# Sparse-attention phase of a hybrid decoder step: packed weights for the prompt blocks, head columns copied tile by tile, first prompt units amid the gate rows, decode softmax in quarters

## The reference

```python
h = rms_norm(x, prm['norm_g'])
p_m, p_n, p_r, p_c = _split(h @ prm['w_in'], GROUP_SIZES)
y_m, ... = mlstm_mixer(p_m, ...)        # group A: matrix memory
y_n, ... = nsa_mixer(p_n, ...)          # group B: sparse attention
y_r, ... = rwkv_mixer(p_r, ...)         # group C: RWKV-7
y_c = memory_mixer(p_c, mem_kv, prm)    # group D: cross attention to 256 memory tokens
y = jnp.concatenate([y_m, y_n, y_r, y_c], -1) @ prm['w_out']
return x + y, ...
```

```python
for r in range(R):                       # R = 2 halves of a block of 32
    hid = hid + jnp.einsum('bnshcd,csde->bnhce', sub[:, r:r + n_cmp],
                           w1[:, r * CMP_STRIDE:(r + 1) * CMP_STRIDE])
kv = jnp.einsum('bnhce,ced->bnhcd', jax.nn.gelu(hid), prm['nsa_cmp_w2'])
...
e = jnp.exp(s - jnp.where(jnp.isfinite(m), m, 0.0))
return e / jnp.maximum(jnp.sum(e, -1, keepdims=True), 1e-30)
...
o = gt[:, :, 0] * o_cmp + gt[:, :, 1] * o_slc + gt[:, :, 2] * o_win
out = o.reshape(B, T, GW).astype(p.dtype) * jax.nn.silu(z)
```

## Time and profile before

| | us |
|---|---|
| median of three runs (lowest, highest) | 1641.11 (1629.98, 1643.89) |
| profiled execution, its own time | 1643.66 |
| span in the profile | 1642.0 |
| PE busy | 1446.8 (88%) |
| DVE busy | 809.4 (49%) |
| ACT busy | 406.2 (25%) |
| POOL busy | 169.3 (10%) |
| chain that ended last, by engine | PE 72%, DVE 11%, issue 8%, SP queue 3%, ACT 2%, DMA 2% |
| granted TensorE clock, mean | 0.895 |

### The profile page before, as it was taken

One profiled execution on the slowest core, in us unless ns is written; L12 is line 12 of the kernel. 1 busy time (PEld: TensorE's weight loads), 2 busy tenths in 40 slices (PEclk: granted clock), 3 DMA queues, 4 the chain that ended last, 5 costly groups with the idle time before them and its releaser, 6 DMA issues.

```text
span 1642.0 us, 28050 instructions
## 1 busy us (share of the span) xinstructions
PE 1446.8 (88%) x9880; PEld 1032.9 (63%) x9880; DVE 809.4 (49%) x2006; ACT 406.2 (25%) x783; POOL 169.3 (10%) x312
## 2 busy tenths in 40 slices
PE   5998989889998988678999899999989989877787
PEld 3774877888854765354458377788877548644443
DVE  1445557665455635742125466665463475266411
ACT  4230102111112344530332110121110124336300
POOL 0000000000000263220000000000000003651100
PEclk9987899996799988899999779999586989888999
DMA  7132322510031465255242233131100404571611
GB/s 298 66 105 65 135 86 65 168 52 1 1 136 60 131 175 184 74 206 216 77 157 77 80 103 132 52 105 78 52 2 1 160 35 152 155 236 33 245 65 64
DMA packets 93216, 175.91 MB, mean 107 GB/s; under 512 B 14114, under 2 KB 79827, under 8 KB 86931
## 3 DMA queue, kind: packets, MB, share of 16 engines
q1 hardware_dynamic: 80066, 124.58, 22.9%
q0 software_dynamic: 13008, 49.54, 8.6%
HBM read 161.27 MB, written 21.12 MB: 111 GB/s over the span
## 4 chain that ended last, share of the span: by engine, by line
PE 72%; DVE 11%; issue 8%; SPq 3%; ACT 2%; DMA 2%; POOL 0%; POOLq 0%; DVEq 0%; ACTq 0%
PE bank L581 16%; PE bank L618 12%; PE bank L1186 8%; PE bank L2743 3%; PE bank L514 2%; PE bank L1320 2%; SPq L387 2%; PE bank L2259 2%; PE bank L814 1%; PE bank L1212 1%; PE bank L1308 1%; PE bank L1297 1%; PE bank L2283 1%; DMA stream<-in_slcV 1%; DVE area L1663 1%
## 5 line engine op out<-in xcount | busy, mean ns | idle before, releaser
L581 PE MATMUL bank<-stream,hT 128*128 128x512 f32 (+3 forms) x768 | 266.9, 505 | 14.6 <-ACT area L594 14.1
L618 PE MATMUL bank<-hT,stream 128*128 128x272 f32 x960 | 229.8, 401 | 5.1 <-DVE area L1552 5.1
L581 PEld LDWEIGHTS bank<-stream,hT 128*128 128x128 f32 x768 | 148.4, 197 | 117.1 <-issue 103.2
L618 PEld LDWEIGHTS bank<-hT,stream 128*128 128x128 f32 x960 | 185.6, 194 | 44.8 <-DVE area L1552 5.3
L1186 PE MATMUL bank<-stream,prm 128*128 128x256 f32 x512 | 127.5, 412 | 0.4 <-DVE YT L1533 0.4
L2743 PE MATMUL bank<-stream,YT 128*128 128x512 f32 x256 | 114.3, 608 | 5.6 <-DVE YT L2651 5.6
L1186 PEld LDWEIGHTS bank<-stream,prm 128*128 128x128 f32 x512 | 105.8, 209 | 18.3 <-issue 1.4
L2259 PE MATMUL bank<-cst,hT 128*128 128x128 f32 x224 | 44.7, 318 | 55.1 <-DVE hT L2715 54.5
L2743 PEld LDWEIGHTS bank<-stream,YT 128*128 128x128 f32 x256 | 49.5, 195 | 68.0 <-issue 61.9
L407 POOL DMA_DIRECT2D stream<-in_slcV x128 | 68.8, 542 | 129.7 <-PE bank L2241 68.9
L2259 PEld LDWEIGHTS bank<-cst,hT 128*128 128x128 f32 x224 | 25.4, 150 | 87.4 <-DVE hT L2715 81.9
(11 more groups left out here) (616 smaller groups left out, 2357.9 us busy)
## 6 DMA issues: line engine op xcount, KB each, us to landing
stream<-in_cmpL SPq DMA_DIRECT2D x256, 128.0 KB, 2.3
stream<-in_win_ SPq DMA_DIRECT2D x12, 2048.0 KB, 8.0
stream<-in_slcK SPq DMA_DIRECT2D x128, 64.0 KB, 2.3
stream<-in_slcK POOLq DMA_DIRECT2D x128, 64.0 KB, 2.5
stream<-in_slcV SPq DMA_DIRECT2D x128, 64.0 KB, 2.6
stream<-in_slcV POOLq DMA_DIRECT2D x128, 64.0 KB, 2.7
stream<-in_wout SPq DMA_DIRECT2D x4, 2048.0 KB, 9.0
out_winpast<-in_winraw POOLq DMA_DIRECT2D x2, 4064.0 KB, 26.6
```

The costliest lines, as they stand in the source:

```text
L581: last = nc.tensor.matmul(ps[:, 0:w], hT[:, k, tok(i)], ws[:, k, :], start=(k == 0), stop=(k == KT - 1))
L618: last = nc.tensor.matmul(ps[:, 0:HALF], ws[:, k, 128 * f:128 * f + 128], hT[:, k, HALF * s:HALF * s + HALF], start=(k == 0), stop=(k == K ...
```

## The change

It has four parts.

1. **Packed weights.** The weights `w1p`, which the decode pages are compressed with already, serve the prompt blocks too. `KVT` holds pairs of neighbouring tokens in the two halves of the partitions, and 8 matmuls take the place of 16 for each of keys and values. w1f is no longer streamed.
2. **Heads by tile.** ACT copies T3 tile by tile (`act_take_heads`), tile 0 in phase R, behind a new wait for the store of the shift rows (`so`); the others ahead of the barrier. The memset of the tail rows and the GELU of `HIDD` move into phase R. PE does `pe_r_end` before the last tile of T3.
3. **First units amid the gate rows.** Scores of units 0 and 1 come before F3's fourth row block, and their maxima and exponentials are taken there; units 0 and 1 get buffers of their own. The selection of the decode blocks comes later on DVE.
4. **Decode softmax.** DVE masks the selected scores by quarters, each with its maximum (`dve_decode_mask`), at units 0, 1, 3 and 4. ACT takes the exponential in three steps at units 5 to 7. The selected scores are no longer scaled before the transposes; instead the value products are scaled as they are added. Window scores move to unit 1, memory scores to unit 3, turns to `TSTEP`, values to a new `VSTEP`.

POOL's loads of slcK 0 and 1 come ahead of its stores of new cache rows.

```diff
-            items += [("w", l, n) for n in ("T2", "T3", "T4", "T5")] + [("w1f", l), ("w", l, "F3")]
+            items += [("w", l, n) for n in ("T2", "T3", "T4", "T5", "F3")]
@@ pool_r
-            pool.dma(f"stR{l}", pool.eng.dma_start(io["rsh"][l], SHO).then_inc(stored["R"][l], 16))
+            pool.dma(f"so{l}", pool.eng.dma_start(io["rsh"][l], SHO).then_inc(shift_stored[l], 16), "so", l)
@@ act_r
             act(nc.scalar.copy(TK, bank("dtk", l)[:, 0:128]).then_inc(act_done, 1), "TK", l)
+            act.wait_ge(dve_done, at("HID", l, DB - 1))
+            act.wait_ge(dve_done, at("peb", l))
+            for c in range(2):
+                act(nc.scalar.activation(HIDD[:, :, c, :], HIDD[:, :, c, :], ACT.Gelu_apprx_tanh, bias=peb[:, c:c + 1]).then_inc(act_done, 1), "G", l)
...
+            act.wait_ge(shift_stored[l], at("so", l))
+            act.wait_ge(pe_done, at("full", "dbn", l))
+            act.wait_ge(dve_done, at("ntails", l))
+            act_take_heads(act, l, 0)
             act.wait_ge(dve_done, at("v20", l))
@@ dve_r
             dve_r_dec(dve, l)
+            dve(nc.vector.memset(PN[:, 4, 0:1166], 0.0).then_inc(dve_done, 1), "ntails", l)
             dve_r_norm(dve, l)
@@ pool_n
+            pool_pages(pool, "slcK", l, 0)
+            pool_pages(pool, "slcK", l, 1)
             pool.wait_ge(act_done, at("PT4", l))
...
-            for kind in ("slcK", "slcV"):
-                for c in range(4):
-                    pool_pages(pool, kind, l, c)
+            pool_pages(pool, "slcK", l, 2)
+            pool_pages(pool, "slcK", l, 3)
+            for c in range(4):
+                pool_pages(pool, "slcV", l, c)
@@ pe_n
-            pe_project_tm(pe, l, "T3")
-            pe_r_end(pe, l)
+            pe.wait_ge(sem_of_slot("w", l, "T3"), at("here", "w", l, "T3"))
+            for i in range(TILES):
+                if i == 4:
+                    pe_r_end(pe, l)
+                pe_project_tile(pe, l, "T3", i)
+            pe.name("used", "w", l, "T3")
...
-            pe_project_rows(pe, l, "F3", 3)
+            pe.wait_ge(dve_done, at("fbk", l))
+            pe_unit_s(pe, l, 0)
+            pe_unit_s(pe, l, 1)
+            pe_project_rows(pe, l, "F3", 3, (4, 5))
             pe_decode_blocks(pe, l)
-            pe_decode_scores(pe, l, 3)
+            pe_decode_scores(pe, l, 3, 7)
@@ pe_block_hidden
             for c in range(2):
-                for s in range(16):
-                    last = nc.tensor.matmul(ps[:, 64 * c:64 * c + 64], wf[:, c, s, :], kv[:, c, :, :, s], start=(s == 0), stop=(s == 15))
+                for j in range(8):
+                    last = nc.tensor.matmul(ps[:, 64 * c:64 * c + 64], w1p[:, c, j, :], KVT[:, c, :, :, j], start=(j == 0), stop=(j == 7))
@@ pe_decode_turn
             if k < 4:
-                pe.wait_ge(dve_done, at("SBn", l))
+                pe.wait_ge(act_done, at("EMe", l, k // 2))
@@ pe_decode_step
-            if u == 3:
+            if u == 1:
                 pe_decode_near(pe, l)
-            elif u == 5:
+            elif u == 3:
                 pe_decode_mem(pe, l)
-            elif 8 <= u < 14:
-                pe_decode_turn(pe, l, u - 8)
+            elif u in TSTEP:
+                pe_decode_turn(pe, l, TSTEP.index(u))
             elif u in VSTEP:
                 pe_decode_values(pe, l, VSTEP.index(u))
-        VSTEP = (14, 15, 16, 18, 20, 22)
+        TSTEP = (7, 8, 9, 10, 14, 15)
+        VSTEP = (11, 12, 13, 16, 17, 19)
@@ act_n
+            for i in range(1, TILES):
+                act_take_heads(act, l, i)
             barrier(act, ("R", l))
...
-            take_project_tm(act, l, "T3", PN[:, :, 0:512], nc.scalar.copy)
...
+            act_unit_e(act, l, 0)
+            act_unit_e(act, l, 1)
             act_gate_rows(act, l, 3)
             act_decode_scores(act, l, 3)
-            act_unit_e(act, l, 0)
-            act_unit_e(act, l, 1)
+        def act_take_heads(act, l, i):
+            act.wait_ge(pe_done, at("full", "T3", l, i))
+            ps = bank("T3", l, i)
+            if i < 4:
+                act(nc.scalar.copy(PN[:, i, 0:512], ps[:, :]).then_inc(act_done, 1), "PT3", l, i)
+            else:
+                for j in range(4):
+                    act(nc.scalar.copy(PN[0:DTOK, 4, 128 * j:128 * j + 128], ps[32 * j:32 * j + 32, 0:128]).then_inc(act_done, 1), "PT3", l, i)
+            act.free("T3", l, i)
@@ act_decode_step
-            if u == 6:
+            if 5 <= u < 8:
                 act.wait_ge(dve_done, at("dm", l))
-                for c, x in enumerate((SB, EW, EM_)):
-                    act(nc.scalar.activation(x, x, ACT.Exp, bias=dm4[:, c:c + 1], accum_out=ds4[:, c:c + 1]).then_inc(act_done, 1), "EMe", l)
+                for part in ((0,), (1,), (2, 3))[u - 5]:
+                    x, c = ((SB[:, 0:1024], 0), (SB[:, 1024:2080], 0), (EW, 1), (EM_, 2))[part]
+                    act(nc.scalar.activation(x, x, ACT.Exp, bias=dm4[:, c:c + 1], accum_out=ds4[:, part:part + 1]).then_inc(act_done, 1), "EMe", l, part)
@@ dve_n
                 for h in range(2):
-                    dve(nc.vector.tensor_copy(KVT[half(h), c, h, :], ps[half(h), :]).then_inc(dve_done, 1), "KVT", l)
+                    src = ps[half(h), :].rearrange("p (n j q) -> p n j q", j=8, q=2)
+                    for q in range(2):
+                        dve(nc.vector.tensor_copy(KVT[half(q), c, h], src[:, :, :, q]).then_inc(dve_done, 1), "KVT", l)
@@ dve_decode_mask
+        def dve_decode_mask(dve, l, c):
+            dve.wait_ge(act_done, at("DS", l, c))
+            sb, off = SB[:, 512 * c:512 * c + 512], bc(BI[:, 8 * c:8 * c + 8], 2, SLC_BLOCK)
+            sb3 = sb.rearrange("p (n j) -> p n j", j=SLC_BLOCK)
+            dve(nc.vector.tensor_tensor(sb3, sb3, off, ALU.add).then_inc(dve_done, 1))
+            dve(nc.vector.reduce_max(DMX[:, c:c + 1], sb, axis=AX.X).then_inc(dve_done, 1))
@@ dve_decode_step
+            if u == 0:
+                dve(nc.vector.memset(DMX, -1e30).then_inc(dve_done, 1))
+                dve_decode_mask(dve, l, 0)
+            elif u == 1:
+                dve_decode_mask(dve, l, 1)
+            elif u == 2:
...
+                dve(nc.vector.tensor_copy(EW[:, 0:512], ps[:, :]).then_inc(dve_done, 1))
+                dve(nc.vector.reduce_max(DMX[:, 5:6], ps[:, :], axis=AX.X).then_inc(dve_done, 1))
...
+            elif u == 9:
+                dve.wait_ge(act_done, at("EMe", l, 3))
+                dve(nc.vector.tensor_tensor(ds4[:, 1:2], ds4[:, 0:1], ds4[:, 1:2], ALU.add).then_inc(dve_done, 1))
+                dve(nc.vector.reciprocal(ds4[:, 1:4], ds4[:, 1:4]).then_inc(dve_done, 1))
+                dve(nc.vector.tensor_tensor(ds4[:, 1:3], ds4[:, 1:3], G3[:, 1:3], ALU.mult).then_inc(dve_done, 1))
+                dve(nc.vector.tensor_scalar(EW, EW, ds4[:, 2:3], None, ALU.mult).then_inc(dve_done, 1))
+                dve(nc.vector.tensor_scalar(SB[:, 2048:2080], SB[:, 2048:2080], ds4[:, 1:2], None, ALU.mult).then_inc(dve_done, 1), "EWn", l)
...
-                    dve(nc.vector.tensor_tensor(ORN, ps[:, 0:256], ORN, ALU.add).then_inc(dve_done, 1))
+                    dve(nc.vector.scalar_tensor_tensor(ORN, ps[:, 0:256], ds4[:, 1:2], ORN, ALU.mult, ALU.add).then_inc(dve_done, 1))
@@ dve_prompt
-            dve_decode_blocks(dve, l)
+            dve_unit_m(dve, l, 0)
+            dve_unit_m(dve, l, 1)
             dve.wait_ge(act_done, at("PCe", l))
...
-            dve_unit_m(dve, l, 0)
-            dve_unit_m(dve, l, 1)
             dve_unit_p(dve, l, 0)
+            dve_decode_blocks(dve, l)
```

More of the change, by code:

```diff
@@ L158 @@
 }
-INS = ["const", "prm", "x", "memx", "wmem", "win_", "wout", "w1f", "ptab", "cmpL", "slcK", "slcV", "winK", "memK",
+INS = ["const", "prm", "x", "memx", "wmem", "win_", "wout", "ptab", "cmpL", "slcK", "slcV", "winK", "memK",
        "winV", "memV", "winraw",
@@ L260, in build @@
         names += [f"xt{i}" for i in range(TILES)]
[L261 removed]
+        names += [f"{a}{l}" for a in ("xr", "ys", "so") for l in range(DEPTH)]
         names += [f"{a}{g}{l}" for a in ("st", "ld") for g in "EMRN" for l in range(DEPTH)]
@@ L2382, in act_unit_e @@
                 act.wait_ge(dve_done, at("UM", l, u, h))
-                act(nc.scalar.activation(PB[u % 2][h][:, 0:n], bank("us", l, u, h)[:, 0:n], ACT.Exp, bias=pm2[u % 2][:, h:h + 1], scale=-1.0,
+                act(nc.scalar.activation(PB[u if u < 2 else 2 + u % 2][h][:, 0:n], bank("us", l, u, h)[:, 0:n], ACT.Exp, bias=pm2[u % 2][:, h:h + 1], scale=-1.0,
                                        accum_out=ps2[u % 2][:, h:h + 1]).then_inc(act_done, 1), "UE", l, u, h)
@@ L2427, in dve_n @@
             dve.name("nss", l)
-            for a in (VBD, HIDP, KVT, QNZ, QRZ, QMZ0, QMZ1, QN2):
+            for a in (VBD, HIDP, QNZ, QRZ, QMZ0, QMZ1, QN2):
                 dve(nc.vector.memset(a, 0.0).then_inc(dve_done, 1))
@@ L2597, in dve_decode_step @@
         def dve_decode_step(dve, l, u):
-            if u == 1:
-                dve_decode_mask(dve, l)
+            if u == 0:
```

(12 more changed lines are left out.)

84 lines of the change are left out of this document (33 added, 51 removed).

## The result

The changed kernel takes 1573.43 us, the median of four runs (1568.88 to 1578.01); the kernel before took 1635.55 beside it (four runs, 1628.01 to 1643.89). The ratio is 0.9619, with a 95% interval of 0.955 to 0.9688. The forecast was 1564 us, from 77.8 us of gain; 62.1 were measured. Medians in this document take all executions of a kernel; the ratios leave out those more than 1.5% above its fastest (one each of e1 and e10, two of e11). The direction, the range and most steps held. One term, the prompt stretch, gave half of its 21.1 us a layer. Parts are numbered here as in the prediction: 1 is the heads, 2 the packed weights, 3 the stream and its pages, 4 the prompt stretch with units 0 and 1 and the decode softmax.

The account below looks back on a forecast made before the run. In the prompt stretch no engine is full; time goes in waiting in turn, with PE (busy 88% overall) the floor. Terms 8.9 + 1.6 + 7.3 + 21.1 = 38.9 a layer, 77.8 for two, gave 1564 us; range 1546 to 1602.

Parts of the forecast that it names:

- Part 1: Heads copied early: PE's 7.1 us wait before T4 goes and T4's first tile takes 1.8 less; 8.9 a layer.
- Part 2: Prompt block compression: 32 of 64 instructions go (3.7 us), but PE then waits 2.1 for the GELU; 1.6 a layer.
- Part 3: Stream with one item fewer: the 5.54 us wait at slcK1 goes and its scores take 1.8 less; 7.3 a layer.
- rival of locked-out descriptors: VectorE's two-port instructions delay POOL's slcK loads 0.42 at each of 32 issues; PE waits 1.5 a layer, 1567 us; 4%.
- Part 4: The prompt stretch of the attention phase: terms (a) to (e) together gain 21.1 us a layer.
- the floor: Prompt stretch of 115.2 us: PE's busy time there, 82 us, taken as the least it can last.
- (a): Units 0 and 1 amid the gate rows: waits at lines 2223 and 2243 and first small ones go; 4.2 a layer.
- (b): Decode softmax spread over units: 14.1 us of PE's waits go, less 2.7 at unit 5 and some 2; 9.4 gained.
- (c): Window scores moved from unit 3 to unit 1: PE newly waits 2.4 us for winK, ends 0 and 7.6.
- (d): Decode values start at unit 11 instead of 14: of the 5.84 us wait at slcV3 1.4 remains; 4.4 gained.
- the forecast's rival: Round robin between DMA queues: POOL's 64 KB loads not behind SP's 4 MB, no stall at slcV3; 1561 us; 3%.
- (e): Clock in the prompt stretch (0.87 granted) rises as waits go: 5.5 us a layer, ends 1.7 and 7.

Follow-up runs that it names:

- e1: The kernel before with only the heads part of the change (T3 copied tile by tile, GELU and tail clearing in phase R); 1607.65 us.
- e10: e3 with only the decode window scores moved from unit 1 to unit 2; 1556.9 us.
- e11: e3 unaltered, run again for five rounds on one chip beside the changed kernel; 1555.0 us.
- e3: The changed kernel with each decode copy taken in the unit of PE's step, behind VectorE's scaling and ScalarE's exponentials, not one unit later; 1549.5 us.
- e8: e3 with units 0 and 1 put back behind the gate rows and the last decode quarter, still in their own buffers; 1553.1 us.
- e2: The changed kernel with its fourth part undone (units 0 and 1, decode softmax, steps and copies as before); 1596.89 us.
- e7: e3 with POOL's page loads of the first two slcK quarters back behind the cmp, slc and win stores; 1564.15 us.

## Why the prediction was right, and where it was not

**Part 1** (8.9): the compression starts 9.26 earlier, at 558.30 instead of 567.56. T4's first tile has its 7.13. The waits for the store and the memset cost nothing. Right.

**Part 2** (1.6): from the compression's start to the use of its GELU it was 16.96 and is 15.44, so 1.5; 32 instructions, and the wait of 1.78 for 2.1 forecast. Right, the lost cover included.

**Part 3** (7.3): the marker comes 20.3 earlier, of which 9.3 and 1.5 are accounted for: 9.5. The wait of 5.54 went and the scores took 1.72 less, as forecast. Another 1.7 is in the memory heads' transposes (line 2022: 2.33 at a clock of 1.00; before, line 2002: 4.04 at 0.54), and whether it is this part's stays open: e1 still waits 5.85 for the second quarter, yet has 2.33 there. The rival of locked-out descriptors would have had PE wait 1.5 at the second quarter, by the rule of the Trainium skill, SBUF — State Buffer (Who interferes with whom), named there. All of POOL's slcK issues in the changed kernel, those beside VectorE's head norms among them (ns, min/median/max):

```profile
L407 POOL DMA_DIRECT2D stream<-in_slcK x128: 537/537/1034, 538.7 to 1358.6; - x128
```

Single issues are longer (1034 at most, 558 before), the median is what it was, the mean 552 where it was 537, and PE waits for none. A delay of 0.42 at each, which that rival put on them, is not there.

**Part 4** (21.1): 10.8 by the markers. The forecast's own sign of being wrong, that unit 0 to the end of the phase stays over 105, came true by a little. The stretch was 115.2 and is

```profile
614.80:721.10 106.30, 80.60 (x840) 48.66 (x838) 66.20 (x210) 51.20 (x133) 35.09 (x66) 0.89 0.70 239
```

In e3 it is 89.9, with PE busy 75.6: so the 82 that the forecast called the floor is none: the same work took 6 less at a clock of 0.92 for 0.87.

- (a) Units 0 and 1 (4.2): the waits at lines 2223 and 2243 went, all but 0.3 of 2.9; with e8's 2.1 and 1.9, half to two thirds of the term. The small waits inside the stretch did not go: unit 1 waits 2.73 for its first probabilities.
- (b) The decode softmax was undersized, not over: the waits at scaled probabilities fell by 17.6 a layer (54.5 to 19.2), where 14.1 less 2.7 and 2, that is 9.4, were forecast, and 1.3 in (a). The forecast's sign, 54.5 to about 22, does not follow from these terms, which leave 33. Unit 5 waits 3.28 (2.7 forecast).
- **The failed step is in (b):** the twelve copies moved from the unit of their step to the next were not costed ("small delays ... some 2"). They are 13.3 a layer, so that (b) gave 4.3 and not 9.4. The prediction followed VectorE's sum and the exponentials, and did not ask who waits for a step that is moved later; its answer was in the code, where every one of these steps opens bank 6.
- (c) The window scores: a wait of 1.73 and 1.3 at the lower clock (3.22 for 1.92) for 2.4 forecast. Near in size, but e10 shows that removing it alone gains nothing.
- (d) The stall of 5.8 at slcV3 went; the forecast had left 1.4. But e2 has values at the old units and no stall in layer 0; e7 has them early and a stall of 4.8. By e7 the order of POOL's queue decides it, and the forecast gave it no term. By the round-robin rule of the Trainium skill, DMA: Bandwidth & Descriptors (SWDGE vs HWDGE vs iDMA), the forecast's rival had no stall left. In e7 there is one, and POOL's 64 KB loads take up to 9.8 beside SP's 4 MB, 2.2 at the least. How the DMA engines shared their turns no run here shows.
- (e) The clock's 5.5 came to 0.2 (busy 100.0 to 99.8). With the bank waits gone it is there: e3 has 94.8, 5.2 less than the kernel before, at 0.91 for 0.88.

The idle time closes: 17.6 and 5.8 gone, 2.6 at lines 2223 and 2243 gone, 13.3 and 1.7 come: 11.0, where the busy rows show 10.6. With the copies in their own unit the stretch gives 27.2 and 29.6 a layer against the kernel before, slcV3's stall included, and 24.2 and 22.8 against e2, more than the 21.1 forecast: the mechanism was there and its last hand-over was misplaced.

That the total came within 10 us of the forecast is in part luck. Besides the 13.3 a layer for bank 6 it missed things both ways: 8.2 too little on the softmax's waits, the order of POOL's queue, some 2.5 a layer more up to the marker, 5.2 lost at the end, and a clock in the R stage that moves by 15 between executions.

## What to carry to other kernels

When a step is moved in a hand-ordered pipeline, list for each of its results who takes it, where in that engine's order the taking stands, and when the producer wants the buffer again. Put the taking right behind the last work that cannot wait for the step, in the same unit: one unit later cost 13 us of waits a layer here, 15 to 18 by the markers, and a place too early in the unit 7 to 9. A stall at a DMA can be set by the order of unrelated transfers over 100 us earlier in the same queue, so try the order by itself, and look at the end of the kernel too. Where the clock moves by itself, compare the stretch that was changed, not only the whole.

## What was not expected of the hardware

- The same 1078 matmuls take 112.9, 124.0 or 128.3 us in executions of like kernels, at clocks of 0.83, 0.74 and 0.70, and few values between; in layer 0 of one and the same kernel 112.9 and 119.8.
- POOL pauses 2.40 us between two loads of one quarter in kernels that issue the cmp, slc and win stores ahead of the slcK pages, and not in those that issue them behind; these take 5 us more from the last store's issue to the end.
- Seven waits of 0.2 to 3.3 us at the bank, 13.3 in all, cost more than their own length: with them the stretch had a clock of 0.88, with 2.1 of them left 0.91, worth 5.0 of busy time.
